# Two MLPs of a streaming encoder: from slabs that alternate hidden and output matmuls to two passes over inner rows in DRAM, with Strassen's seven products in both matmuls

## The reference

```python
def sq_relu_ffn(h, w1, w2):            # w1: 1024 x 4096, w2: 4096 x 1024
    return jnp.square(jax.nn.relu(h @ w1)) @ w2
...
    f_p = sq_relu_ffn(modulated_norm(x_p, norm2_g[i], sh2_p, sc2_p), ffn_w1[i], ffn_w2[i])
    x_p = x_p + gt2_p[:, None, :] * f_p
```

## Time and profile before

| | us |
|---|---|
| median of 3 runs | 2819.53 |
| range of the runs | 2818.36 to 2819.55 |
| span of the profiled execution, first to last instruction | 2818.3 |
| PE busy | 2724.4 (97%) |
| DVE busy | 1834.6 (65%) |
| ACT busy | 1142.0 (41%) |
| POOL busy | 871.5 (31%) |

### The profile page before, as it was taken

One profiled execution on the slowest core, in us unless ns is written; L12 is line 12 of the kernel. 1 busy time (PEld: TensorE's weight loads), 2 busy tenths in 40 slices (PEclk: granted clock), 3 DMA queues, 4 the chain that ended last, 5 costly groups with the idle time before them and its releaser, 6 DMA issues.

```text
span 2818.3 us, 46654 instructions
## 1 busy us (share of the span) xinstructions
PE 2724.4 (97%) x15908; PEld 2445.2 (87%) x15908; DVE 1834.6 (65%) x3066; ACT 1142.0 (41%) x2416; POOL 871.5 (31%) x928
## 2 busy tenths in 40 slices
PE   6989999899999999999999999999999999999998
PEld 4978877799988899999999997888899999999997
DVE  4577777655565767676767775224667676767675
ACT  3355555445552334343434323223244343434331
POOL 1122012056660023434343352000003433334344
PEclk8999999899999999999999999999999999999999
DMA  6244334322244211111111167124421111111118
GB/s 236 80 157 155 133 129 147 112 79 67 72 160 142 98 45 45 45 45 45 45 45 45 60 150 210 37 84 153 139 83 45 45 45 45 45 45 45 45 60 149
DMA packets 122349, 254.09 MB, mean 90 GB/s; under 512 B 15636, under 2 KB 64948, under 8 KB 118904
## 3 DMA queue, kind: packets, MB, share of 16 engines
q1 hardware_dynamic: 116136, 230.19, 24.6%
q0 software_dynamic: 6096, 22.35, 4.0%
HBM read 211.59 MB, written 40.90 MB: 90 GB/s over the span
## 4 chain that ended last, share of the span: by engine, by line
PE 65%; POOL 1%; DMA 1%; DVE 1%; issue 1%; ACT 0%; SPq 0%; POOLq 0%; DVEq 0%; ACTq 0%
PE psum L112 21%; PE psum L110 21%; PE psum L111 21%; POOL half_acc L2649 1%; PE psum L3109 1%; PE psum L3250 1%; DMA scratch_x_mid<-half_acc 0%; DMA gate_wv_raw<-in_cm_w_in 0%; PE psum L3261 0%; PE psum L3224 0%; DMA half_m<-scratch_mixT 0%; DVE half_out L2862 0%; DVE half_w_lo L2731 0%; DVE gate_x L2994 0%; DVE gate_x L2997 0%
## 5 line engine op out<-in xcount | busy, mean ns | idle before, releaser
L110 PE MATMUL psum<-half_hT_hi,half_w_hi 128*128 128x384 f32 x1536 | 513.7, 334 | 0.0
L112 PE MATMUL psum<-half_hT_hi,half_w_lo 128*128 128x384 f32 x1536 | 513.4, 334 | 0.0
L111 PE MATMUL psum<-half_hT_lo,half_w_hi 128*128 128x384 f32 x1536 | 513.3, 334 | 0.0
L2613 POOL TENSOR_TENSOR half_acc<-half_acc,half_upd 128x512 f32<-128x512 f32 x312 | 422.9, 1373 | 33.6 <-ACT half_upd L2382 28.9
L112 PE MATMUL psum<-half_w_hi,half_s_lo 128*128 128x512 f32 x1040 | 405.7, 390 | 0.0
L111 PE MATMUL psum<-half_w_lo,half_s_hi 128*128 128x512 f32 x1040 | 405.6, 390 | 0.0
L110 PE MATMUL psum<-half_w_hi,half_s_hi 128*128 128x512 f32 x1040 | 405.3, 390 | 0.0
L2829 DVE TENSOR_TENSOR half_acc<-half_acc,psum 128x512 f32<-128x512 f32 x416 | 279.2, 681 | 81.0 <-PE psum L112 81.0
L2365 ACT ACTIVATE half_s_raw<-psum 128x384 f32<-128x384 f32 (+2 forms) x256 | 97.7, 407 | 563.5 <-PE psum L112 563.5
L110 PEld LDWEIGHTS psum<-half_hT_hi,half_w_hi 128*128 128x128 f32 x1536 | 288.3, 188 | 1.2
L111 PEld LDWEIGHTS psum<-half_hT_lo,half_w_hi 128*128 128x128 f32 x1536 | 288.3, 188 | 1.2
(11 more groups left out here) (384 smaller groups left out, 5729.9 us busy)
## 6 DMA issues: line engine op xcount, KB each, us to landing
half_w_raw<-in_w SPq DMA_DIRECT2D x64, 512.0 KB, 4.2
half_w_raw<-in_w SPq DMA_DIRECT2D x128, 256.0 KB, 3.5
patt_mod_w<-in_ada_w_ffn SPq DMA_DIRECT2D x32, 768.0 KB
patt_mod_w<-in_ada_w_att SPq DMA_DIRECT2D x16, 1024.0 KB, 4.9
half_m<-scratch_mixT SPq DMA_DIRECT2D x18, 512.0 KB, 5.1
satt_lT_raw<-in_cacheT SPq DMA_DIRECT2D x32, 256.0 KB, 3.0
satt_l_raw<-in_cache SPq DMA_DIRECT2D x32, 256.0 KB, 2.9
half_w_raw<-in_w_o SPq DMA_DIRECT2D x16, 512.0 KB, 5.3
```

Source lines behind the costliest of these rows:

```text
L110: pe.matmul(out, a_hi, b_hi, start=first, stop=False)
L111: pe.matmul(out, a_hi, b_lo, start=False, stop=False)
L112: return pe.matmul(out, a_lo, b_hi, start=False, stop=last)
L2613: pool.tensor_tensor(part, part, a.upd[n % UPDS][:], ALU.add).then_inc(a.added, 1)
```

## The change

Each MLP becomes two passes. The first pass makes all hidden rows, two inner tiles (a `Pair`) at a time, now with seven products too: the 2x2 blocks are (two inner tiles, two halves of the k-tiles) by (two halves of the k-tiles, two blocks of GN = 288 tokens), and there are two such groups of tokens. A pair is 14 units of 4 x 3 matmuls 288 wide, 168 in all, and there are 16 pairs to a layer. The right factor's seven blocks of h are made and split once per layer and stay in SBUF; the sums of w1 are made per pair by POOL (`w1_sums`). The products are chained in PSUM: P1, P6, P7, P4 go on adding into one bank, P5 and P3 into a second, P2 has a third; ACT takes copies of the chain on the way (`take_hidden`) and DVE adds the other bank to the copy (`read_hidden`). Relu and square are one DVE instruction (`square`), and the squared rows (a `piece`, 576 KB) go to a DRAM tensor `hid`.

The second pass makes the output, over slabs of four inner tiles (SLABS = 8) by four pairs of token tiles (a step). It loads the left factor from `hid` (512 KB a step), POOL makes its sums (`s_sums`), ACT and DVE split it, w2 is loaded as 2 x 1 MB a slab and its sums are made by DVE (`w2_sums`). A step is seven products of 2 x 3 matmuls 512 wide; the sample tile has 24 more per slab. The accumulators are now the four blocks themselves, not the seven products, so there is no joining and no plain slab. The loop over steps is written out, not a loop on the chip. Three of the four blocks of a step need an addition by POOL (`add`) besides DVE's (`read`).

Below is the core of the diff: the orders of products, SP's two passes, ACT's, POOL's and DVE's functions of the passes, and PE's.

```diff
-PAIRS = TT // 2
...
+S1, S2, S4 = range(4, 7)
 S3 = A21
-B11, B21, B22, T1, T2, B12, T4 = range(7)
+P1, P2, P3, P4, P5, P6, P7 = range(7)
...
+H_FACTORS = {P1: (A11, HB11), P2: (A12, HB21), P3: (S4, HB22), P4: (A22, HT4),
+             P5: (S1, HT1), P6: (S2, HT2), P7: (S3, HT3)}
+H_ORDER = (P1, P5, P6, P2, P7, P4, P3)
+H_ORDER1 = (P1, P2, P5, P6, P7, P4, P3)
+UNITS = 2 * len(H_ORDER)
...
-P2, P3, P4, P7, P1, P6, P5 = range(7)
 FACTORS = {P1: (A11, B11), P2: (A12, B21), P3: (S4, B22), P4: (A22, T4), P5: (S1, T1), P6: (S2, T2), P7: (S3, T3)}
-JOBS = (P1, P6, P2, P3, P7, P4, P5)
-READ, EVICTED = JOBS[0::2], JOBS[1::2]
-N_READ, N_EVICT, N_JOBS = 4 * PAIRS + 2, 3 * PAIRS, 7 * PAIRS + 2
-PLAIN = 2
...
+            def load_w1(a, i, ahead):
+                par = (i.par + ahead) % 2
+                sp.dma_start(a.w_q[par][:].rearrange("p (f s) n -> p f (s n)", f=2), w1_pairs[a.layer][i.index(1, ahead)]
+                             ).then_inc(a.c.w1_in[par], 16)
+
+            def store_piece(a, i, f):
+                sp.wait_ge(a.c.sq_ready, i.count(2, 2 - f))
+                sp.dma_start(hid[i.index(2, f)], a.piece[i.par][f][:].rearrange("p a b n -> p (a b n)")
+                             ).then_inc(a.c.piece_stored[i.par][f], 16)
+
+            def load_w2(a, i, e):
+                u = w2_unit(i, e)
+                sp.dma_start(a.w_q[u][:].rearrange("p (f s) n -> p f (s n)", f=2), w2_pairs[a.layer][2 * (i % SLABS) + e]
+                             ).then_inc(a.c.w2_in[e], 16)
...
+            def load_s(a, n):
+                i, j = n // PAIRS, n % PAIRS
+                if j == 0:
+                    hidden_stored(a, i)
+                if n % STEPS >= 3:
+                    sp.wait_ge(a.c.f_ready, pair_end(n - 3))
+                r = s_place(a, n)[0]
+                sp.dma_start(a.s_q[r][:].rearrange("p e f n -> p (e f) n"),
+                             hid_slabs[i % SLABS, :, :, 2 * j * P:2 * (j + 1) * P]).then_inc(a.c.s_in[r], 16)
...
+                with sp.Fori(0, FFS // 2 - 1) as m:
+                    for i in (Pair(a, 1, m), Pair(a, 2, m)):
+                        sp.wait_ge(a.c.hid_ready, i.count(UNITS))
+                        load_w1(a, i, 1)
+                        store_piece(a, i, 1)
+                        store_piece(a, i, 0)
+                i = Pair(a, FFS - 1)
+                sp.wait_ge(a.c.hid_ready, i.count(UNITS))
+                slab = SLABS * a.layer
+                load_w2(a, slab, 0)
+                sp.wait_ge(a.c.hid_ready, unit_done(i, P5, 1))
+                load_w2(a, slab, 1)
+                for n, product in enumerate((P6, P2, P7)):
+                    sp.wait_ge(a.c.hid_ready, unit_done(i, product, 1))
+                    load_s(a, PAIRS * slab + n)
+                store_piece(a, i, 1)
+                store_piece(a, i, 0)
+                sp.wait_ge(a.c.hid_ready, i.count(UNITS, UNITS))
+                sp.wait_ge(a.c.hid_read, hid_reads(i, 3))
+                load_s8(a, slab)
...
+            def output_steps(a):
+                for i in slabs_of(a):
+                    if i % SLABS:
+                        sp.wait_ge(a.c.f_ready, i * N_JOBS)
+                        load_s8(a, i)
+                    if i % SLABS < LAST:
+                        load_w2(a, i + 1, 0)
+                        load_w2(a, i + 1, 1)
+                    else:
...
+                    for j in range(PAIRS):
+                        n = PAIRS * i + j
+                        if n % STEPS + 3 < STEPS:
+                            load_s(a, n + 3)
...
+            def take(a, n, m):
+                i, j = n // PAIRS, n % PAIRS
+                product, c = ((P1, C11), (P6, C12), (P7, C22))[m]
+                act.wait_ge(a.c.f_ready, job(n, product))
...
+                else:
+                    k = 3 * n + m
+                    if i % SLABS:
+                        act.wait_ge(a.c.added, 3 * n - (3, 1, 2)[m])
+                    out = a.tmp[k % 4][:]
+                act.activation(out, psum[:, o_bank_of(product, j), :], ACT.Copy).then_inc(a.c.taken, 1)
+
+            def output_steps(a, extra=lambda j, place: None):
+                for n in steps_of(a):
+                    i, j = n // PAIRS, n % PAIRS
+                    last, more = i % SLABS == LAST, (n + 1) % STEPS > 0
+                    take(a, n, 0)
+                    if more:
+                        s_hi_q(a, n + 1)
+                    else:
+                        extra(j, 0)
+                    take(a, n, 1)
+                    if more:
+                        s_hi_r(a, n + 1)
+                    if not last and j in (1, 2):
+                        w2_hi_q(a, i + 1, j - 1, 0)
+                    if last:
+                        extra(j, 1)
+                    take(a, n, 2)
+                    if not last and j in (1, 2):
+                        w2_hi_q(a, i + 1, j - 1, 1)
+                        w2_hi_r(a, i + 1, j - 1)
+                    if j == 1:
+                        s8_hi(a, i)
+                    if last:
+                        extra(j, 2)
...
+            def w1_sums(a, i, ahead):
+                par = (i.par + ahead) % 2
+                q, r = a.w_q[par], a.w_r[par]
+                s1, s2, s4 = (r[:, s - 4, :] for s in (S1, S2, S4))
+                pool.wait_ge(a.c.w1_in[par], i.times(ahead) + 16)
+                pool.tensor_tensor(q[:, S3, :], q[:, A21, :], q[:, A11, :], ALU.subtract).then_inc(a.c.w1_sum, 1)
+                pool.wait_ge(a.c.w1_sum, i.count(4, 4 * ahead + 1))
+                pool.tensor_tensor(s2, q[:, S3, :], q[:, A22, :], ALU.add).then_inc(a.c.w1_sum, 1)
+                pool.wait_ge(a.c.w1_sum, i.count(4, 4 * ahead + 2))
+                pool.tensor_tensor(s1, s2, q[:, A11, :], ALU.add).then_inc(a.c.w1_sum, 1)
+                pool.tensor_tensor(s4, q[:, A12, :], s2, ALU.subtract).then_inc(a.c.w1_sum, 1)
...
+            def s_sums(a, n):
+                ring, loaded = s_place(a, n)
+                q, r = a.s_q[ring], a.s_r[ring]
+                s1, s2, s4 = (r[:, :, s - 4, :] for s in (S1, S2, S4))
+                x11, x12, x21, x22 = (s_slots(q, s) for s in (A11, A12, A21, A22))
+                pool.wait_ge(a.c.s_in[ring], loaded)
+                pool.tensor_tensor(x21, x21, x11, ALU.subtract).then_inc(a.c.s_sum, 1)
+                pool.wait_ge(a.c.s_sum, 4 * n + 1)
+                pool.tensor_tensor(s2, x21, x22, ALU.add).then_inc(a.c.s_sum, 1)
+                pool.wait_ge(a.c.s_sum, 4 * n + 2)
+                pool.tensor_tensor(s1, s2, x11, ALU.add).then_inc(a.c.s_sum, 1)
+                pool.tensor_tensor(s4, x12, s2, ALU.subtract).then_inc(a.c.s_sum, 1)
...
+            def add(a, n, m):
+                i, j = n // PAIRS, n % PAIRS
+                c = (C11, C12, C22)[m]
+                part = acc_part(a, j, c)
+                pool.wait_ge(a.c.taken, 3 * n + m + 1)
+                if m != 1:
+                    pool.wait_ge(a.c.read, read_done(n, c))
+                pool.tensor_tensor(part, part, a.tmp[(3 * n + m) % 4][:], ALU.add).then_inc(a.c.added, 1 if i % SLABS else 3)
...
+            def output_steps(a, extra=lambda j, place: None):
+                for n in steps_of(a):
+                    i, j = n // PAIRS, n % PAIRS
+                    last = i % SLABS == LAST
+                    if i % SLABS:
+                        add(a, n, 1)
+                        add(a, n, 0)
+                    if last:
+                        extra(j, 0)
+                    add(a, n, 2)
+                    if last:
+                        extra(j, 1)
+                    if n % STEPS + 2 < STEPS:
+                        s_sums(a, n + 2)
+                    if j == 0:
+                        s8_sum(a, i)
+                    if last:
+                        store_tile(a, 2 * j)
+                        store_tile(a, 2 * j + 1)
...
+            def hidden_step(a, i):
+                both = (0, 1)
+                if i.last:
+                    slab, n = SLABS * a.layer, STEPS * a.layer
+                    w2_sums(a, slab, 0)
+                    read_hidden(a, i, C11, both)
+                    w2_lo_q(a, slab, 0)
+                    read_hidden(a, i, C22, both)
+                    w2_sums(a, slab, 1)
+                    w2_lo_r(a, slab, 0)
+                    s_lo_q(a, n)
+                    w2_lo_q(a, slab, 1)
+                    read_hidden(a, i, C12, both)
+                    s_lo_r(a, n)
+                    w2_lo_r(a, slab, 1)
+                    square(a, i, 1)
+                    square(a, i, 0)
+                    return
+                read_hidden(a, i, C11, both)
+                w1_lo_q(a, i, 1)
+                read_hidden(a, i, C22, both)
+                w1_lo_r(a, i, 1)
+                square(a, i, 1)
+                read_hidden(a, i, C12, both)
+                square(a, i, 0)
...
+            def w2_sums(a, i, e):
+                u, q = w2_unit(i, e), 2 * i + e
+                w, r = a.w_q[u], a.w_r[u]
```

(89 more changed lines are left out.)

1404 lines of the change are left out of this document (712 added, 692 removed).

## The result

The changed kernel takes 2891.07 us in the median of 4 runs (2889.2 to 2895.44), the kernel before 2819.49 beside it: a ratio of 1.026 (1.0245 to 1.0274), slower by 2.6%. The forecast was 2803.5 us, so the miss is 88 us, and the time lies 49 us beyond the upper end of the range (2842). The profiled execution has a span of 2893.8 us, against 2818.3 before: 75.5 us more.

What follows compares the result with a forecast made beforehand. PE was taken to bound the kernel. 2818.3 - 93.2 + 5 + 54 + 10 + 4 + 3 + 1.2 = 2802.3 us span, 2803.5 as median with 1.2 added; the 8-in-10 range was 2755 to 2842.

Steps and rivals of the forecast that it cites:

- What PE saves: Matmuls of both MLP layers: hidden 41.1 us and output 5.5 us less per layer, 93.2 us in all.
- The hidden pass: First MLP pass: w1's chain fits a 22.4 us pair with 1.3 us to spare; 5 us charged over 28 pairs.
- rival (c): Hidden pass: w1 lands late in each of 28 pairs, costing 48 us instead of 5, so 2846; chance 0.12.
- The output pass: Second MLP pass: DVE and POOL hold each other up, 4.0 us a slab in slabs 1 to 6, 54 us for two layers.
- exclusion: Output pass: DVE operations with two SBUF operands and POOL's go by turns, DVE's PSUM reads excepted; 2 to 4.4 us a slab.
- 51 us of claims on shared time: Output-pass slab: DVE 23 plus POOL 28 us, less start-up, hence 43 to 51 in a slab of 43.6.
- tally of one slab: Output pass: one slab followed by turns, PE waiting in steps 2 and 3 for DVE's reads and splits, 4.3 us.
- the bound in which nothing overlaps: Output pass: upper bound of the loss per slab, 51 - 43.6 = 7.4 us.
- Slabs 0 and 7: Output pass: lighter first slab (one POOL add per step, 2 us) and last slab (no w2 work, 1 us).
- rival (b): Output pass: DVE and POOL block each other more strongly; 7.4 us in each slab is 118, time 2868; chance 0.16.
- Projection to hidden: Turn into the hidden pass: second group's h summed and split within the first group's 11 us; 2 us a layer, 4 us.
- Hidden to output: Turn between MLP passes: DVE's w2 work queues behind the last pair; PE waits 5 us a layer (2 to 9), 10 us.
- Gate handover: Turn to the gate: x returns from DRAM, DVE work precedes the turned rows; 3 us more wait than before (-9 to +12).

## Why the prediction failed, by its steps

**What PE saves**: right. 168 matmuls of 288 columns in 22.40 us are 0.1333 each, for 0.1334 forecast; a pair takes the 22.40 us that were named.

**The hidden pass**: right that it fits; the 5 us charged did not come. W1's 1 MB lands 5.9 us after issue (taken 6). But rival (c), W1 late, does occur in one place that the prediction did not look at, the second pair, which is 4.1 and 3.0 us too long.

**The output pass**: the mechanism, exclusion as the earlier trace rows had it, was right; the size was not. This is the first step that failed. 51 us of claims on shared time were set against 43.6, with start-up time taken off, and a tally of one slab gave 4.3; I took 4.0. Measured are 6.3, nearer to 7.4, the bound in which nothing overlaps. Taking claims away confirms it from two sides, the second with the reservation made above: with the adds nearly emptied a slab takes 44.55, with POOL's 16 sums gone 45.2. What the tally left out is how the delays go round: DVE's split of W2 holds its read of P2, the read holds POOL's add, the add holds POOL's sums of the next rows, the sums hold ACT's split, and ACT's copies of P6 and P7 stand behind that split. PE's largest wait, 9.8 us in six slabs, is for these copies; the prediction named only DVE's reads and splits. Moving the one split of W2 shows 2.7 of the 6.3 to be of this kind. Putting ACT's copies ahead of its splits would be the direct test and was not run, so how the other 3.6 divide between claims and queue order stays open. Slabs 0 and 7 were taken for light at 3 us a layer; they have 12.6 and 8.5. In slab 7 DVE has the scalings in place of W2's work, 2 x 1.22 us a step, again with two SBUF operands, and in the first layer splits of the gate's weights; I had noted only what is absent. The term is 97 where 54 stood (93 without the gate's share), so it is rival (b) in kind, short of its 118.

**Projection to hidden**: the step that failed worst, 4 for 47. I took the 7 splits of the second group to fit into the 11 us of the first but for 2 us, and did not count DVE's whole queue: over the first pair DVE is busy for 33.2 of 36.7 us, with 22.4 of matmuls. Nor did I count the 5.5 us ahead of the pair in each layer, in which the last norm runs beside POOL's splits. The runs show that neither POOL's splits ahead of the norm nor its sums of W1 set the end: taking a stall away moved most of it on, and all the edits together took 3.0 and 4.9 us off the way to the first pair's end (42.8 and 43.0 in the changed kernel). That DVE's own load bounds the pair is argued from its busy time (35.7 of 37.5 us in the second layer, once POOL's splits are gone and its sums moved) and these shifts; no run took it away. The price of the lower granted clock in that pair, 0.90 to 0.93 on the mean in the changed kernel, is in the 47 and was not in the forecast.

**Hidden to output**: 15 for 10, inside its bounds of 4 to 18.

**Gate handover**: 11.9 us more than before, for 3: inside the bound of 12, but only just. Of the old 8.4 us in the last slab 3.9 stayed, and 16.4 us came behind the pass. PE is busy for 30.5 of the first 44 us, where the kernel before was busy for 43.8 of 44.6, and DVE for only 22.4, with the DMA engines at 0.80 of the time. Emptying POOL's adds left 352.5 us for the stretch, for 355.2 in the changed kernel, so POOL's adds are 2.7 of it at most; reordering DVE's queue moved 2.3 us of waits from the turned rows to the weights and saved none. Their loads wait for memory that the output pass frees at its end, which points to them, but no run moved them: this stays open.
